# The opening of a two-part transformer: its first modulated features regrouped by fours, handed on one k-tile at a time

## The chip, the cores and the metric

The kernel runs on one core of a Trainium2 chip. The metric is device time in microseconds (us), from the first to the last instruction of the program plus what lies around them. Lower is better.

## The reference, cut to what matters

The program is a chain of two blocks on a sequence of 256 rows of 1024 features. The first block has two layers of adaptive modulation, a hybrid attention and a gated feed-forward part, the second two layers with attention and a squared-ReLU part. Only the very first steps are touched by the change:

```python
def rmsnorm(x, g):
    y = xf * lax.rsqrt(jnp.mean(xf * xf, axis=-1, keepdims=True) + RMS_EPS)
    return (y * g).astype(x.dtype)

cos, sin = rope_tables(positions)
cond = jax.nn.silu(c)
for l in range(DEPTH):
    mod = (cond @ ada_w[l] + ada_b[l])[:, None, :]
    sh1, sc1, g1, sh2, sc2, g2 = jnp.split(mod, 6, axis=-1)
    h = rmsnorm(x, norm1_g[l]) * (1 + sc1) + sh1
    x = x + g1 * hybrid_mixer(h, cos, sin, w_in[l], b_in[l], rel_bias[l], ...)   # starts with h @ w_in + b_in
    ...
```

Here `c` is one row of 1024, `ada_w[l]` is 1024 x 6144, `w_in[l]` is 1024 x 6733, and `h` is 256 x 1024. So the first product `h @ w_in` can't start before the row `cond @ ada_w` has given the shift (`sh1`) and the scale (`sc1`) of the features that it takes.

## The kernel before, in words

**Numbers and tiles.** A weight goes to TensorE as two rounded parts. ACT (ScalarE) copies a unit of the weight (two k-tiles of 128 rows, up to 512 columns) from `raw_units` to `hi_units` (line 1305), and POOL (GpSimd) writes the rest, raw minus hi, to `lo_units`, one k-tile at a time (line 730). The features are held turned (features on partitions) in `turned`, also as a hi and a lo part. Per k-tile and 128-row tile there are three matmuls (line 776): hi by hi, lo by hi, hi by lo. A unit is thus 12 matmuls, 8 on `hi_units` and 4 on `lo_units`. The eight input chunks of the first product are 458 columns wide; a chunk is 4 units. Chunks use two pairs of PSUM banks in turn, so the third chunk waits until DVE (VectorE) has drained the first (line 2025).

**Where the data comes from.** SP (SyncE) issues nearly all loads in one fixed order, the list `stream` of `plan()`: units of `ada_w` and of the weights, woven. Units of `w_in` go to 8 slots, and a slot is free when POOL has made its lo part.

**The opening.** The modulation of the first norm consists of four pieces of 512 features: scale0, shift0, scale1, shift1 (0 for features 0 to 511, 1 for the rest), each 4 units of 2 k-tiles of `ada_w`. DVE adds up the k-tiles of a piece over the partitions' own rows, one instruction of 128 x 512 each (lines 1714, 1717, 1720), the last one to `mod_rows`. The second unit of scale1 is left to TensorE (`PE_UNITS`, line 1113). Then TensorE adds over partitions and turns the sum to columns at once, with four matmuls of one column for a piece (`column_sums`, line 1123); an f32 matmul shows in the trace as two instructions. The bias row and the norm's gain are loaded as rows to one partition, and turned to columns with matmuls of one row (lines 1104 and 1097). The bias row of three pieces also enters DVE's first sum of a piece (line 1714), so it is loaded over memsets of POOL and DVE.

ACT meanwhile squares `x`, takes the root, and writes x over the root mean square to `o_rows` (`unit_rows`, line 1355), which TensorE transposes (line 909). `first_columns` (DVE, line 1794 on) and `first_hi` (ACT, line 1336 on) then scale and shift the turned features, two k-tiles at once: DVE scales the first pair, ACT the second, ACT makes the hi parts (line 1347), DVE the lo parts (line 1768), and TensorE starts on a pair when its lo part is there. Both run once for each half. Between the halves TensorE multiplies the first half's features with two units of chunk 0, and one or two units of chunk 1. The rotary angles and the table of the relative bias are made by DVE and ACT after the second half (`tables`, `angles`, lines 1945 to 1975; sine, line 1532).

`keep_running` (line 1131) issues full-width matmuls whose result nobody reads; it only gives TensorE something to do.

**Order.** Nothing is scheduled by a planner here: each engine's order is the order of its code, and engines wait on semaphores for named events. `sums_upto(n)` lets DVE go through the modulation units up to the nth.

## Time and profile before

| | us |
|---|---|
| median of 3 runs (1469.13 to 1471.74) | 1470.4 |
| the profiled execution | 1470.62 |
| its span, first to last instruction | 1468.8 |
| TensorE (PE) busy | 1443.4 (98%) |
| GpSimd (POOL) busy | 1198.3 (82%) |
| ScalarE (ACT) busy | 748.1 (51%) |
| VectorE (DVE) busy | 727.8 (50%) |

The profiled execution lasts 1.8 us longer than its span, and 0.2 us longer than the median of the runs. PE is busy for nearly the whole span, so idle time of another engine matters only where PE waits for it. The engines' shares are means over the whole program; the change concerns only its first 57 us.

### The profile page before, as it was taken

What the parts mean: (1) busy time and instruction counts of PE and PEld (TensorE: products, weight loads), DVE (VectorE), ACT (ScalarE), POOL (GpSimd) and SP (SyncE); (2) the same over time, 40 slices, a digit from 0 to 9 for tenths busy, and PEclk for the clock granted to TensorE, in tenths of its full rate; (3) what the DMA queues carried; (4) which work ended last, traced back from release to release, by engine and by line L of the source; (5) the groups of instructions that cost most, each with busy time, mean ns of one, the idle gap of its engine ahead of it and who ended that gap; (6) DMA issues with size and microseconds to landing.
All of it is one profiled execution on the core that took longest, in us unless ns stands there. A gap on an engine that the chain in (4) does not pass through costs nothing.

```text
span 1468.8 us, 21705 instructions
## 1 busy us (share of the span) xinstructions
PE 1443.4 (98%) x7684; PEld 1217.0 (83%) x7684; DVE 727.8 (50%) x1579; ACT 748.1 (51%) x1246; POOL 1198.3 (82%) x974
## 2 busy tenths in 40 slices
PE   7999999999999999999999999999999999999997
PEld 5898777899988988777888888888888888788886
DVE  7863654776634654745566214364650044655202
ACT  4435774644444445765544445465654345555441
POOL 2799989888878987558998989908999978489994
PEclk8999999999999999999999999999999999999999
DMA  9994557678885995337775665714566757256561
GB/s 362 387 357 158 188 177 225 230 299 309 306 276 184 398 313 182 116 102 235 235 247 183 192 204 169 230 43 157 190 199 199 217 157 223 65 171 201 190 201 55
DMA packets 149416, 313.37 MB, mean 213 GB/s; under 512 B 10918, under 2 KB 31802, under 8 KB 149307
## 3 DMA queue, kind: packets, MB, share of 16 engines
...
## 4 chain that ended last, share of the span: by engine, by line
PE 92%; DVE 4%; ACT 2%; POOL 1%; issue 1%; DMA 1%; SPq 0%; DVEq 0%; ACTq 0%
PE bank L776 57%; PE bank L821 12%; PE bank L822 8%; PE bank L819 5%; PE bank L1006 2%; PE bank L986 1%; PE bank L1022 1%; POOL lo_units L730 1%; PE bank L857 1%; PE bank L966 1%; DMA x_rows<-in_x 1%; PE bank L1009 1%; PE bank L953 1%; ACT hi_units L1305 0%; PE bank L955 0%
## 5 line engine op out<-in xcount | busy, mean ns | idle before, releaser
L730 POOL TENSOR_TENSOR lo_units<-raw_units,hi_units 128x512 fp32r<-128x512 f32 (+3 forms) x928 | 1151.2, 1279 | 243.9 <-ACT hi_units L1305 241.2
L1305 ACT ACTIVATE hi_units<-raw_units 128x1024 fp32r<-128x1024 f32 (+1 forms) x468 | 480.5, 1031 | 424.2 <-PE bank L776 262.8
L776 PE MATMUL bank<-hi_units,turned 128*128 128x512 f32 (+3 forms) x1600 | 439.1, 389 | 2.1 <-DVE turned L1768 1.3
L776 PEld LDWEIGHTS bank<-hi_units,turned 128*128 128x128 f32 x1600 | 293.0, 189 | 53.8 <-DVE turned L1768 2.9
L822 PE MATMUL bank<-turned,lo_units 128*128 128x256 f32 x1024 | 287.9, 281 | 0.0
L776 PE MATMUL bank<-hi_units,turned_wide 128*128 128x512 f32 x992 | 274.5, 391 | 0.0
L821 PE MATMUL bank<-turned,hi_units 128*128 128x512 f32 x736 | 258.7, 396 | 0.0
L776 PE MATMUL bank<-lo_units,turned 128*128 128x512 f32 (+3 forms) x800 | 253.3, 384 | 0.8 <-POOL lo_units L730 0.5
L776 PEld LDWEIGHTS bank<-hi_units,turned_wide 128*128 128x128 f32 x992 | 185.3, 188 | 38.5 <-issue 0.5
L822 PEld LDWEIGHTS bank<-turned,lo_units 128*128 128x128 f32 x1024 | 194.3, 190 | 0.2
L776 PEld LDWEIGHTS bank<-lo_units,turned 128*128 128x128 f32 x800 | 150.0, 188 | 30.4 <-POOL lo_units L730 3.6
L821 PEld LDWEIGHTS bank<-turned,hi_units 128*128 128x128 f32 x736 | 138.1, 188 | 32.7
L776 PE MATMUL bank<-lo_units,turned_wide 128*128 128x512 f32 x496 | 160.7, 389 | 0.0
L1720 DVE SCALAR_TENSOR_TENSOR bank<-ada_units,small,bank 128x512 f32<-128x512 f32 x148 | 111.8, 756 | 33.7 <-DMA ada_units<-in_ada_w 28.9
L776 PEld LDWEIGHTS bank<-lo_units,turned_wide 128*128 128x128 f32 x496 | 93.1, 188 | 19.6
L1786 DVE TENSOR_REDUCE bank<-bank 128x256 f32<-128x512 f32 x92 | 64.3, 699 | 84.3 <-PE bank L822 83.6
L819 PE MATMUL bank<-turned,hi_units 128*128 128x256 f32 x576 | 104.0, 283 | 0.0
L819 PEld LDWEIGHTS bank<-turned,hi_units 128*128 128x128 f32 x576 | 90.2, 192 | 0.6
L1652 ACT ACTIVATE mlp_relu<-bank 128x256 f32<-128x256 f32 x56 | 21.6, 386 | 59.4 <-DVE bank L1786 58.8
L2213 DVE SCALAR_TENSOR_TENSOR bank<-x_rows,bank 128x512 f32<-128x512 f32 x8 | 5.2, 693 | 88.8 <-PE bank L776 88.8
L1782 DVE TENSOR_TENSOR turned_wide<-bank,turned_wide 128x256 fp32r<-128x256 f32 x92 | 39.0, 424 | 14.6 <-ACT turned_wide L1367 11.8
L2226 DVE SCALAR_TENSOR_TENSOR bank<-x_rows,bank 128x512 f32<-128x512 f32 x8 | 5.6, 696 | 75.8 <-PE bank L776 75.6
...
## 6 DMA issues: line engine op xcount, KB each, us to landing
...
```

The costliest lines, as they stand in the source:

```text
L730: pool.tensor_tensor(LO[:, s, b, 0:w], RAW[:, u["slot"], b, 0:w], HI_[:, s, b, 0:w].bitcast(F32), ALU.subtract).then_inc(lo_ready.sem, lo_ ...
L776: ins = pe.matmul(BANK[2 * c["pair"] + t][:, 0:w], (A[a] if A is BT else A[:, a])[:, part, t * P:(t + 1) * P], W[:, s, b, 0:w], start=(i = ...
L819: pe.matmul(bank[:, 0:S], HI_[:, s, b, at:at + P], A[:, kt, part, :], start=kt == 0 and part == 0, stop=False)
L821: pe.matmul(bank[:, :], HI_[:, s, b, at:at + P], A[:, kt, :, :].rearrange("p two s -> p (two s)"), start=kt == 0, stop=False)
L822: ins = pe.matmul(bank[:, 0:S], LO[:, s, b, at:at + P], A[:, kt, 0, :], start=False, stop=kt == KT - 1)
L857: ins = pe.transpose(BANK[(TQ, TP)[n % 2]][:, j * P:(j + 1) * P], src[:, t, (4 * half + j) * P:(4 * half + j + 1) * P], con("ident"))
L1006: pe.matmul(score_bank(pipe, h + n)[:, 0:S], pipe["qk"][rows_, slot, P:S], kk[rows_, :], start=True, stop=True)
L1305: act.activation(HI_[:, s, 0:n, 0:w], RAW[:, u["slot"], 0:n, 0:w], ACT.Copy)\
L1652: act.activation(RTN[:, m % 4, :], BANK[(TQ, TP)[m % 2]][:, 0:S], ACT.Relu).then_inc(act_side.sem, act_side.mark(("relu tile", i, m)))
L1720: ins = v.scalar_tensor_tensor(total, raw[:, k, :], COND[:, kt:kt + 1], partial, ALU.mult, ALU.add)
L1782: tell(v.tensor_tensor(AT[:, n, 1, :], h, AT[:, n, 0, :].bitcast(F32), ALU.subtract), turned_lo, (tag, "tile", n))
L1786: return v.tensor_reduce(to, bank[:, :].rearrange("p (two s) -> p s two", two=2), AX_X, ALU.add)
```

## The change

- **Fours.** Within a half, k-tile number j (0 to 3) now holds the features 4q + j, q being the partition, instead of 128j + q. The rows of `w_in` of layer 0 are loaded in the same order, `unit_rows` reads x with a step of four elements, and the last sum of each modulation piece is written to `mod_rows` in this order.
- **Columns.** With that, a partition's four biases (and gains) are four neighbours in memory, and two small loads put them into place as columns (`BIAS`, `GAIN`). The bias and gain matmuls, the row tile with its memsets, and the bias in DVE's first sum are gone. `scale_columns` makes the gain column from the sums of a scale piece before the shift piece is there, and `column_sums` of the shift follows it.
- **Scale1's unit on TensorE** is now two matmuls of 512 columns into one row (`sum_row`), which ACT writes to SBUF, regrouped, and four matmuls of one row turn it to columns.
- **Single k-tiles.** `first_hi`, `first_columns` and the new `first_unit` hand over one k-tile at a time; two k-tiles of a half share each of the two banks. All eight transposes of a half are issued together (`first_turn`).
- **Order.** `tables`, `angles`, the sines and the store of the bias table come first on DVE and ACT. On PE, chunk 1's second unit moves ahead of the column sums of shift1. There are 15 `keep_running` matmuls in place of 6.

The diff, cut to its core:

```diff
-                    a = tile_rows(src)[row0:row0 + ((n - 1) * step + 1) * P, col0:col0 + ncols].rearrange("(k p) n -> p k n", p=P)[:, ::step, :]
+                    if src == ("w_in", 0):
+
+                        half, j = divmod(row0 // P, 4)
+                        a = tile_rows(src)[half * CW:(half + 1) * CW, col0:col0 + ncols].rearrange("(q j) n -> q j n", j=4)[:, j:j + n, :]
+                    else:
+                        a = tile_rows(src)[row0:row0 + ((n - 1) * step + 1) * P, col0:col0 + ncols].rearrange("(k p) n -> p k n", p=P)[:, ::step, :]
...
-        def column_products(c, i):
+        def sum_row(c, i):
 
             u = c["units"][i]
             pe.wait_ge(ada_in[u["home"]][u["slot"]], 16 * (u["turn"] + 1))
             for k in range(UNIT_K):
+                kt = i * UNIT_K + k
+                ins = pe.matmul(BANK[3][0:1, :], COND[:, kt:kt + 1], ada_raw(u)[:, k, :], start=k == 0, stop=k == UNIT_K - 1)
             ins.then_inc(ada_multiplied.sem, ada_multiplied.mark(u["index"]))
...
             pe.wait_ge(ada_used.sem, ada_used.at(c["units"][-1]["index"]))
+            if n == 3:
+                for j in range(4):
+                    pe.matmul(columns[:, at + j:at + j + 1], SUM_ROW[0:1, j * P:(j + 1) * P], ONES[0:1, 0:1], start=j == 0, stop=False)
+            if n < 2:
+                pe.wait_ge(rows.sem, rows.at(("scales", half)))
             for j in range(4):
                 ins = pe.matmul(columns[:, at + j:at + j + 1], MOD[:, n * CW + j * P:n * CW + (j + 1) * P], ONES[:, 0:1],
-                                start=False, stop=n < 2 and j == 3)
-            if n < 2:
-                ins.then_inc(product.sem, product.mark(("columns", half)))
-
-        def keep_running(n):
+                                start=n != 3 and j == 0, stop=j == 3)
+            ins.then_inc(product.sem, product.mark(("columns", n)))
...
+        def first_turn(half):
+
+            pe.wait_ge(act_side.sem, act_side.at(("unit rows", half)))
+            if half:
+                for k in (2, 3):
+                    pe.wait_ge(turned_lo.sem, turned_lo.at((("n1", 0), k)))
+            for k in range(4 * half, 4 * half + 4):
+                for t in range(NT):
+                    at = k % 4 // 2 * S + t * P
+                    ins = pe.transpose(BANK[(TQ, TP)[k % 2]][:, at:at + P], O[:, t, k * P:(k + 1) * P], con("ident"))
...
+        def first_unit(c, i):
+
+            for m in range(UNIT_K):
+                pe.wait_ge(turned_lo.sem, turned_lo.at((("n1", 0), i * UNIT_K + m)))
+                unit(c, i, HT, only=m)
...
-        keep_running(1)
-        pe.wait_ge(first_gain_in, 16)
-        gain_columns(0)
-        pe.wait_ge(first_bias_in, 16)
-        bias_columns(scale0)
-        keep_running(2)
+        keep_running(6)
         column_sums(scale0)
+        keep_running(4)
...
-                ready = lambda g: (act_side, ("unit rows", g // 2))
-                turn(tag, O, range(4), 0, ready)
-                turn(tag, O, range(4), 1, ready)
+                first_turn(0)
                 keep_running(1)
                 column_sums(shift0)
                 keep_running(2)
-                for i in (0, 1):
-                    pe.wait_ge(turned_lo.sem, turned_lo.at((tag, i)))
-                    unit(c0, i, HT)
-                turn(tag, O, range(4), 2, ready)
-                turn(tag, O, range(4), 3, ready)
-                pe.wait_ge(rows.sem, rows.at(("columns", 0)))
-                gain_columns(1)
-                column_products(scale1, 1)
+                first_unit(c0, 0)
+                first_unit(c0, 1)
+                sum_row(scale1, 1)
+                first_turn(1)
+                pe.wait_ge(act_side.sem, act_side.at("sum row"))
                 unit(c1, 0, HT)
                 column_sums(scale1)
+                unit(c1, 1, HT)
                 column_sums(shift1)
-                unit(c1, 1, HT)
-                for c in (c0, c1):
-                    for i in (2, 3):
-                        pe.wait_ge(turned_lo.sem, turned_lo.at((tag, i)))
-                        unit(c, i, HT)
+                keep_running(2, BANK[SB_[0]])
+                first_unit(c0, 2)
+                first_unit(c0, 3)
+                unit(c1, 2, HT)
+                unit(c1, 3, HT)
...
+            a, b, c, d = range(4 * half, 4 * half + 4)
+            raw = lambda k: BANK[(TQ, TP)[k % 2]][:, k % 4 // 2 * S:(k % 4 // 2 + 1) * S]
+
+            def whole(k):
+                act.activation(raw(k), raw(k), ACT.Identity, scale=GAINED[:, k:k + 1], bias=SHIFT[:, k:k + 1])\
+                    .then_inc(act_side.sem, act_side.mark(("whole", k)))
+
+            def hi(k, signal_):
+                act.wait_ge(signal_.sem, signal_.at(("whole", k)))
+                act.activation(HT[:, k, 0, :], raw(k), ACT.Copy).then_inc(turned_hi.sem, turned_hi.mark((("n1", 0), k)))
+
+            act.wait_ge(turned.sem, turned.at((("n1", 0), half)))
             act.wait_ge(rows.sem, rows.at(("columns", half)))
+            whole(b)
+            hi(a, rows)
+            hi(b, act_side)
+            hi(c, rows)
+            act.wait_ge(turned_lo.sem, turned_lo.at((("n1", 0), b)))
+            whole(d)
+            hi(d, act_side)
...
-                ins = act.activation(O[:, t, cols], X[:, t, cols], ACT.Copy, scale=RR[:, t:t + 1])
+                ins = act.activation(O[:, t, cols].rearrange("p (j q) -> p j q", j=4), X[:, t, cols].rearrange("p (q j) -> p j q", j=4),
...
+        act.dma_start(GAIN.rearrange("p (h j) -> p h j", h=2), dram["norm1_g"][0:1, :].rearrange("a (h q j) -> (a q) h j", h=2, j=4),
+                      allow_slow_non_contiguous=True).then_inc(first_gain_in, 16)
+        act.dma_start(BIAS.rearrange("p (c j) -> p c j", c=4), dram["ada_b"][0:1, 0:4 * CW].rearrange("a (c q j) -> (a q) c j", c=4, j=4),
+                      allow_slow_non_contiguous=True).then_inc(first_bias_in, 16)
-        act.dma_start(GAIN_ROW, dram["norm1_g"][0:1, :]).then_inc(first_gain_in, 16)
-        act.wait_ge(cleared.sem, cleared.at("second shift"))
-        act.wait_ge(rows.sem, rows.at("cleared"))
-        act.dma_start(FIRST[0:1, :], dram["ada_b"][0:1, 0:4 * CW]).then_inc(first_bias_in, 16)
+        for what, dst in (("sin", SIN), ("cos", COS)):
+            act.wait_ge(rows.sem, rows.at(what))
+            act.activation(dst, dst, ACT.Sin).then_inc(act_side.sem, act_side.mark(what))
+        act.wait_ge(rows.sem, rows.at("rel"))
+        act.dma_start(scratch[:, :], RE[:, :]).then_inc(scratch_in, 16)
...
+                prep(3)
+                act.wait_ge(ada_multiplied.sem, ada_multiplied.at(by_key["ada", 0, 3]["units"][1]["index"]))
+                act.activation(SUM_ROW[0:1, :].rearrange("p (j q) -> p q j", j=4), BANK[3][0:1, :].rearrange("p (q j) -> p q j", j=4), ACT.Copy)\
+                    .then_inc(act_side.sem, act_side.mark("sum row"))
                 prep(NH)
                 first_hi(1)
                 prep(NH + 3)
...
-                    if kt == 0 and (u["l"], u["c"]) in FIRST_BANK and (u["l"], u["c"]) != (0, 2):
-                        dve.wait_ge(cleared.sem, cleared.at("second shift"))
-                        dve.wait_ge(first_bias_in, 16)
-                        link(v.scalar_tensor_tensor(partial, raw[:, k, :], COND[:, kt:kt + 1], FIRST[:, cols], ALU.mult, ALU.add))
-                        continue
                     if kt == 0:
                         link(v.tensor_scalar(partial, raw[:, k, :], COND[:, kt:kt + 1], None, ALU.mult))
                         continue
                     total = MOD[:, cols] if (u["i"], k) == (mine[-1], UNIT_K - 1) and not in_two(u["l"], u["c"]) else partial
+                    if (u["l"], u["c"]) in FIRST_BANK and total is not partial:
+                        by_four = lambda a: a.rearrange("p (q j) -> p q j", j=4)
+                        ins = v.scalar_tensor_tensor(total.rearrange("p (j q) -> p q j", j=4), by_four(raw[:, k, :]), COND[:, kt:kt + 1], by_four(partial),
+                                                     ALU.mult, ALU.add)
...
+            dve.wait_ge(product.sem, product.at(("columns", 2 + half)))
+            dve.wait_ge(first_bias_in, 16)
+            dve.wait_ge(first_gain_in, 16)
+            link(v.scalar_tensor_tensor(GAINED[:, cols], columns[:, at], 1.0, BIAS[:, at], ALU.add, ALU.add))
+            say(v.tensor_tensor(GAINED[:, cols], GAINED[:, cols], GAIN[:, cols], ALU.mult), ("scales", half))
...
         def first_columns(half):
+            a, b, c, d = range(4 * half, 4 * half + 4)
+            raw = lambda k: BANK[(TQ, TP)[k % 2]][:, k % 4 // 2 * S:(k % 4 // 2 + 1) * S]
+
+            def whole(k):
+                say(v.tensor_scalar(raw(k), raw(k), GAINED[:, k:k + 1], SHIFT[:, k:k + 1], ALU.mult, ALU.add), ("whole", k))
+            def lo(k):
+                dve.wait_ge(turned_hi.sem, turned_hi.at((("n1", 0), k)))
+                tell(v.tensor_tensor(HT[:, k, 1, :], raw(k), HT[:, k, 0, :].bitcast(F32), ALU.subtract), turned_lo, (("n1", 0), k))
-            link(v.tensor_copy(GAIN[:, cols], columns[:, 2 * KT + 4 * half:2 * KT + 4 * half + 4]))
-            v.tensor_copy(SHIFT[:, cols], columns[:, cols])
-            say(v.scalar_tensor_tensor(GAINED[:, cols], columns[:, KT + 4 * half:KT + 4 * half + 4], 1.0, GAIN[:, cols], ALU.add, ALU.mult),
-                ("columns", half))
-            g = 2 * half
-            dve.wait_ge(turned.sem, turned.at((("n1", 0), g)))
-            for k in (2 * g, 2 * g + 1):
-                part = BANK[TQ][:, k % 2 * S:(k % 2 + 1) * S]
-                ins = v.tensor_scalar(part, part, GAINED[:, k:k + 1], SHIFT[:, k:k + 1], ALU.mult, ALU.add)
-            say(ins, ("whole", half))
-            turn_lo(("n1", 0), HT, part=slice(2 * half, 2 * half + 2))
+            say(v.tensor_tensor(SHIFT[:, cols], columns[:, cols], BIAS[:, cols], ALU.add), ("columns", half))
+            dve.wait_ge(turned.sem, turned.at((("n1", 0), half)))
+            whole(a)
+            lo(a)
+            lo(b)
+            whole(c)
+            lo(c)
+            lo(d)
...
-        say(v.memset(FIRST[:, 2 * CW:4 * CW], 0.0), "cleared")
...
+        tables()
+        angles()
         sums_upto(5)
+        scale_columns(0)
+        sums_upto(6)
         dve.wait_ge(act_side.sem, act_side.at(("root", ("n1", 0))))
         say(v.reciprocal(RR[:, 0:NT], RSTD), "inverse root")
         sums_upto(8)
         for l in range(DEPTH):
             if l == 0:
                 first_columns(0)
+                sums_upto(13)
+                scale_columns(1)
                 sums_upto(15)
                 first_columns(1)
-                tables()
-                angles()
```

TensorE (PE) from the start of the program to the first products; L1131 and L1139 are `keep_running`, L1123 and L1114 the column sums, L909 and L1127 the transposes. Before:

```order
L1131 MATMUL bank<-ada_units_61,constants 128x512
L1097 MATMUL bank<-ones_rounded,bias_masks 128x1 x4
L1104 MATMUL bank<-ones_rounded,first_biases 128x1 x4
L1131 MATMUL bank<-ada_units_61,constants 128x512 x2
L1123 MATMUL bank<-ones_rounded,mod_rows 128x1 x4
L909 MATMUL bank<-constants,o_rows 128x128 x8
L1131 MATMUL bank<-ada_units_61,constants 128x512
L1123 MATMUL bank<-ones_rounded,mod_rows 128x1 x4
L1131 MATMUL bank<-ada_units_61,constants 128x512 x2
L776 MATMUL bank<-hi_units,turned 128x458 x4
```

The same place on PE, now:

```order
L1139 MATMUL bank<-ada_units_61,constants 128x512 x6
L1114 MATMUL bank<-ones_rounded,mod_rows 128x1 x4
L1139 MATMUL bank<-ada_units_61,constants 128x512 x4
L1127 MATMUL bank<-constants,o_rows 128x128 x8
L1139 MATMUL bank<-ada_units_61,constants 128x512
L1114 MATMUL bank<-ones_rounded,mod_rows 128x1 x4
L1139 MATMUL bank<-ada_units_61,constants 128x512 x2
L776 MATMUL bank<-hi_units,turned 128x458 x4
```

The one-row matmuls for gain and bias are gone, and full-width matmuls without use stand in their place.

DVE at the start; `small` holds all small columns, `rel_extended` is the table of the relative bias. Before:

```order
L1938 MEMSET first_biases 128x1024
L1941 SCALAR_TENSOR_TENSOR small<-small 128x8
L1942 TENSOR_SCALAR small<-small 128x8
L1944 TENSOR_SCALAR ones_rounded<-constants 128x128
L1717 TENSOR_SCALAR bank<-ada_units_61,small 128x512
```

The same place on DVE, now (eight more small rows like the last but one stand before the last):

```order
L1974 TENSOR_SCALAR ones_rounded<-constants 128x128
L1979 TENSOR_SCALAR rel_extended<-rel_rows 10x256
L1980 TENSOR_SCALAR rel_extended<-rel_rows 10x128
L1986 CAST small<-positions_int 128x2
L1988 TENSOR_SCALAR small<-constants,small 128x8 x2
L1995 TENSOR_SCALAR small<-small 128x16
```

The fourteen instructions of the tables and angles stand ahead of the first sum of a modulation piece.

DVE in the second half; the first rows are sums of shift1 and the last of them writes `mod_rows`. Before:

```order
L1720 SCALAR_TENSOR_TENSOR bank<-ada_units_67,small,bank 128x512 x5
L1720 SCALAR_TENSOR_TENSOR mod_rows<-ada_units_67,small,bank 128x512
L1799 COPY small<-bank 128x4
L1800 COPY small<-bank 128x4
L1801 SCALAR_TENSOR_TENSOR small<-bank,small 128x4
```

The same place on DVE, now:

```order
L1734 SCALAR_TENSOR_TENSOR bank<-ada_units_67,small,bank 128x512 x2
L1816 SCALAR_TENSOR_TENSOR small<-bank,small 128x4
L1817 TENSOR_TENSOR small<-small 128x4
L1734 SCALAR_TENSOR_TENSOR bank<-ada_units_67,small,bank 128x512 x3
L1731 SCALAR_TENSOR_TENSOR mod_rows<-ada_units_67,small,bank 128x128x4
L1833 TENSOR_TENSOR small<-bank,small 128x4
L1826 TENSOR_SCALAR bank<-bank,small 128x256
```

`scale_columns` (L1816, L1817) now stands between sums of shift1, and waits there for PE's column sums of scale1.

## Rows read from the trace of the kernel before

**Rows 1.** The page: busy us, share, instructions; granted PE clock by fortieths.

```profile
PE 1443.4 (98%) x7684; PEld 1217.0 (83%) x7684; DVE 727.8 (50%) x1579; ACT 748.1 (51%) x1246; POOL 1198.3 (82%) x974
```

**Rows 2.** Timeline, first 7 us: start, us, engine, line, operation [idle before <-releaser].

```profile
1.36 0.42 ACTq L1504 DMA_DIRECT2D positions_int<-in_positions  x1
1.81 1.28 ACT L1507 ACT_TABLE_LOAD   x1 [1.81 <-issue]
...
3.87 0.23 DVE L1944 TENSOR_SCALAR ones_rounded<-constants 128x128 fp32r<-128x128 f32 x1
...
6.13 0.75 DVE L1717 TENSOR_SCALAR bank<-ada_units,small 128x512 f32<-128x512 f32 x1 [2.04 <-DMA ada_units<-in_ada_w]
```

**Rows 3.** Timeline of the first half, 15 to 25 us.

```profile
15.09 0.95 PE L1123 MATMUL bank<-ones_rounded,mod_rows 128*128 128x1 f32 x8
15.80 2.56 ACT L1355 ACTIVATE o_rows<-x_rows,small 128x512 f32<-128x512 f32 x4 [0.30 <-DVE small L1981]
15.80 3.92 DVE L1720 SCALAR_TENSOR_TENSOR bank<-ada_units,small,bank 128x512 f32<-128x512 f32 x5
17.19 1.09 PE L909 MATMUL bank<-constants,o_rows 128*128 128x128 f32 x8 [1.14 <-ACT o_rows L1355]
19.16 0.97 ACT L1305 ACTIVATE hi_units<-raw_units 128x916 fp32r<-128x916 f32 x1 [0.79 <-DMA raw_units<-in_w_in]
23.00 1.00 DVE L1807 TENSOR_SCALAR bank<-bank,small 128x256 f32<-128x256 f32 x2
```

**Rows 4.** Chain of waits, 20 to 41 us: start, us, what.

```profile
20.56 1.87 PE bank L1123 x8
22.43 3.26 PE bank L1131 x4
25.69 5.07 PE bank L776 x24
30.75 0.88 PE bank L909 x8
...
32.61 1.88 PE bank L1113 x16
34.48 3.89 PE bank L776 x12
38.38 1.98 PE bank L1123 x16
```

**Rows 5.** Timeline, 43 to 57 us.

```profile
43.40 0.72 PEld L776 LDWEIGHTS bank<-hi_units,turned 128*128 128x128 f32 x4 [0.83 <-DVE turned L1768]
47.54 2.23 DVE L1958 TENSOR_SCALAR small<-constants,small 128x8 f32<-128x8 f32 x2
52.20 0.17 DVE L1974 SCALAR_TENSOR_TENSOR small<-small 128x16 f32<-128x16 f32 x1
54.06 6.88 POOL L730 TENSOR_TENSOR lo_units<-raw_units,hi_units 128x458 fp32r<-128x458 f32 x6 [3.19 <-ACT hi_units L1305]
54.10 0.71 PEld L776 LDWEIGHTS bank<-hi_units,turned 128*128 128x128 f32 x4 [0.82 <-DVE proj_rows L2025]
55.30 0.30 PEld L776 LDWEIGHTS bank<-lo_units,turned 128*128 128x128 f32 x2 [0.49 <-POOL lo_units L730]
56.87 0.81 PEld L776 LDWEIGHTS bank<-hi_units,turned 128*128 128x128 f32 x4
```

**Rows 6.** Windows: stretch, length, busy by engine, granted PE clock, DMA share, GB/s.

```profile
18.70:25.00 6.30, 5.51 (x14) 2.88 (x12) 3.40 (x9) 3.90 (x6) 4.50 (x4) 0.50 1.05 405
```

**Rows 7.** DMA, first 6 us: packets, MB, share of 16 engines.

```profile
q10 hardware_dynamic: 294, 0.02, 3.7%
```

**Rows 8.** The page's costliest groups: xcount | busy, mean ns | idle before.

```profile
L1786 DVE TENSOR_REDUCE bank<-bank 128x256 f32<-128x512 f32 x92 | 64.3, 699 | 84.3 <-PE bank L822 83.6
L1652 ACT ACTIVATE mlp_relu<-bank 128x256 f32<-128x256 f32 x56 | 21.6, 386 | 59.4 <-DVE bank L1786 58.8
L1782 DVE TENSOR_TENSOR turned_wide<-bank,turned_wide 128x256 fp32r<-128x256 f32 x92 | 39.0, 424 | 14.6 <-ACT turned_wide L1367 11.8
```

45 lines of the change are left out of this document (10 added, 35 removed).

## The prediction

> **What bounds the kernel now.** I read the page first. PE is busy for 98% of the span, POOL, the next, for 82% [rows 1]. So the place to look is the opening, where PE has little to multiply; what is won there passes on to the end only if it brings PE's unbroken stretch forward. The timeline shows where that stretch begins: PE waits last for the drain of chunk 0 and for a lo part, and from 56.87 us (the second unit of chunk 2) it goes on without a hole [rows 5]. Hence the measure for every step below: when does this same unit begin?
>
> Before it, the chain of waits shows what PE is held by [rows 4]. It waits for the modulation of each half, and fills the time with useless matmuls: the first product starts at 25.69. In the second half the column sums end at 40.36 (38.38 + 1.98), and the next product starts at 43.40 [rows 5]. DVE sums the whole time, 0.785 us an instruction (3.92 for five) [rows 3]. The third view is the granted clock: 0.50 from 18.7 to 25.0 [rows 6], the lower of its two levels (1.2 of 2.4 GHz); PE had been through one-column matmuls and a wait of 1.14 us just before [rows 3].
>
> **The start.** Two loads more are issued on ACT ahead of its first table. One like them takes 0.42, 0.47 with the gap, so the table, at 1.81 before, comes at 2.75, and DVE's last preparing instruction, which ended at 4.10, ends at 5.05 [rows 2]. Then DVE has 14 small instructions. Beside POOL they took 1.11 each (2.23 for two), the later ones 0.17 [rows 5]; POOL is idle this early, so I count 0.21 each with the gap, 2.95. Bounds: 2.4 to 15.6 (14 x 0.17, 14 x 1.11); I take the low side because POOL has no unit yet. DVE's first sum is at 8.0, against 6.13 [rows 2].
>
> The two loads consist of 768 runs of 16 bytes. In the first 6 us 294 packets of ACT's queue took 3.7% of 16 engines, 3.55 us in all, 12 ns each [rows 7]; 768 make 9.2, or 0.6 us for each of the 16. So the data may come 0 to 0.6 later. DVE, itself 1.9 late, is what the first half then waits for, so I take nothing. The memsets and the bias and gain matmuls of the first half that go are worth nothing either: they lay under waits for the modulation.
>
> **First half.** From 8.0: ten sums to 15.85, two small instructions of `scale_columns` (0.4), two sums, the reciprocal (0.2) at 18.0, four sums to 21.15. Before, the last sum ended at 20.5 (five from 15.80 in 3.92, and one more) [rows 3]; the idle 2.04 and the wait for the root that DVE had are what pays for the tables. `unit_rows` starts at 18.05 instead of 15.80 and takes 2.56 [rows 3]; the first half of it is there at 19.35, the transposes (1.09) end at 20.4, one `keep_running` at 21.3, and the column sums at 22.25. Before that was 22.43 [rows 4], no gain. That sum takes the faster clock: column sums cost 0.95 at it and 1.87 at the slower [rows 3, 4]; a `keep_running` is two instructions, 1.63 to 1.7 in the slow stretch (3.26 for four) [rows 4] and half of it in the fast one.
>
> Here the single k-tiles pay. Before, DVE's small ones, two scalings (1.00), two ACT copies of 512 and a lo part lay between the sums and the first product. Now ACT has the two first units to copy (0.97 each [rows 3]) until 22.6, one scaling 0.5, one copy of 256 columns at 0.39 and one lo part of 256 at 0.42 [rows 3, 8]: 24.0, just when two fast `keep_running` end. First product at 24.0 instead of 25.69: 1.7 won. POOL's lo parts (1.15 each: 6.88 for six) [rows 5] are ready from 22.85 on.
>
> **Second half.** PE, one after the other: four k-tiles 5.07 [rows 4], to 29.1; `sum_row`, two f32 matmuls of 512 columns, priced as `keep_running` at the fast clock, 1.7, to 30.8 (bounds 0.8 and 3.4, half and twice); eight transposes, 1.0 (0.88 to 1.09) [rows 3, 4], to 31.8; a unit, 2.5 (half of 5.07), to 34.3; column sums of scale1, now eight matmuls or 16 instructions, 1.98 as for the 16 before [rows 4], to 36.3. DVE meanwhile: its last lo part at 26.7 (the other three k-tiles take 2.7 more), and ten sums, to 34.55. Then it must wait for those columns until 36.3, for 1.8 us, with the last four sums of shift1 queued behind it: this is the new wait. 0.4 for the scale and four sums, 3.14, bring it to 39.9, and PE, which waits for them, has the column sums at 40.85. Before: 40.36. So half a microsecond is lost here, and of the 1.7 nothing is left.
>
> From there: two `keep_running` (1.7), the product at 42.6, against 43.40: 0.8 won by the single k-tiles again. But ACT is held longer: 0.2, two scalings, four copies of 0.39 and its waits for DVE's end 3.9 after the columns; then it copies the unit for k-tiles 6 and 7 until 45.8, where PE wants it at 45.1. Its lo part takes 1.15 more and is wanted after two thirds of a k-tile, 0.83: that is 0.7 and 0.35, 1.05 lost.
>
> **The tables' old place.** They no longer stand between the second half and the drain of chunk 0, nor the sine before ACT's copies. Both waits of PE there go: four units from 43.40 on and one more, at 2.5, would have brought it to 55.9, and it was 56.87, so they cost 0.97 [rows 5]. What is late next is POOL's lo part of chunk 2's first unit, at 53.9 with 54.5 wanted: hidden.
>
> **Sum.** Product at 42.6, 10.0 for four units, 1.05 of stalls, 2.5 for the first unit of chunk 2: 56.15, against 56.87. 0.7 us won. The profiled execution lasts 1470.62, so 1469.9; the median of the runs is 0.2 lower, so 1469.7. A change of 0.2% is 2.9 us, about what a measurement of this kernel can tell from none: the forecast is no change.
>
> **A rule that speaks against it.** `unit_rows` now reads x in steps of 16 bytes, and four last sums write in steps of 512. No SBUF access of this kind is in the trace. The nearest row is L1786, which reads PSUM in steps of 1 KB: 699 ns for 512 elements, as fast as neighbours would be [rows 8]. So I take no cost. Bounds: nothing to twice the duration, 2.56 and 4 x 0.75 more.
>
> The Trainium skill, page "SBUF — State Buffer", section "Door 1: The DMA port swizzle", says that SBUF has lines of 16 bytes, and that an access that crosses to a new line pays. By it each element of `unit_rows` would pay; by the row none does. No run here shows it yet.
>
> **Rivals.**
> - *No new wait (18%).* DVE isn't held for scale1's columns, because PE gets there 1.8 earlier: `sum_row` at its low bound, or the units at less than I count. For it: the sum on PE is long, and each term can be short. Against: these terms are measured rows but for one. It gives 1.8 more: 1467.9.
> - *The clock falls again (20%).* It fell to 1.2 GHz after one-column matmuls and a wait, and from 18.7 on cost 6.3 us at half speed [rows 6]. Such stretches are still there: transposes and column sums from 19.3 to 22.3, and 38.8 to 40.9, where PE waits for DVE. Against: `keep_running` lies between. Price: column sums 0.9 and two `keep_running` 1.7 longer in the first half, 2.6, or about 1.7 in the second. I take 2.1: 1471.8. That the clock would stay low from the start is unlikely: column sums at 15.09 were fast [rows 3], after 3.5 us of full-width work, and now 5 to 10 us of it come first.
> - *Stepped access is slow (12%).* Where: ACT's four `unit_rows` and DVE's last sum of each piece. At twice the duration, two writes put the reciprocal and shift0 0.75 and 1.5 back, `unit_rows` adds 2.56: first product 3.3 later; shift1's last sum adds 0.75. 4.05 on 1469.7 is 1473.75, slower than before by 3.3. It decides from a factor of 1.2 on (all 0.7 gone), and passes 0.2% at 1.9. For it: the rule; against it: L1786.
> - That the change doesn't do what it says I rule out: the order of instructions shows each move.
>
> **How the numbers follow.** Forecast 50%, own range 1468.5 to 1471.0 (the stalls of 1.05 in or out, as much again for the small terms). No new wait 18%, clock 20%, steps 12%. Faster by over 0.2% (under 1467.5): half of the first rival, and the forecast's lower tail, 17%. Slower (over 1473.3): 8% from the steps and 3% from a clock that falls twice, 11%. The rest, 72%, within 0.2%. The range that leaves out two in ten is 1467.2 to 1472.3.
>
> **What would show it.** DVE's fourteen small instructions at 0.2 and a first sum near 8.0; `unit_rows` at 2.56 in all, and the last sums at 0.75; first products near 24.0; an idle time of DVE near 1.8 before `scale_columns(1)`, released by PE; ACT late with one unit at 45; no wait of PE at the start of chunk 2; and that chunk's second unit near 56.15. Wrong it would be if POOL or the loads, which run at 405 GB/s here [rows 6], can't follow a PE that is 0.8 ahead: then a hole opens after 57 us that wasn't there. It would also be wrong if the clock is at 0.5 from 22 to 25 or at 41.

## The result, and the profile after

The changed kernel takes 1475.9 us (median of 20 runs, 1474.5 to 1477.5); the kernel before, beside it, 1471.45 (most runs 1470 to 1473). Ratio 1.0027, 95% interval 1.0019 to 1.0035: about 4 us slower, where 0.7 us faster was forecast and the range ended at 1472.3. The profiled execution has a span of 1473.6 us against 1468.8.

PE's share is what it was, 98% [rows 1], so I look at the opening first:

```profile
PE 1446.2 (98%) x7674; PEld 1214.0 (82%) x7674; DVE 722.8 (49%) x1582; ACT 751.2 (51%) x1251; POOL 1196.2 (81%) x972
```

The timeline of PE after (start, us, engine, line, operation, idle before), the rows that answer to [rows 3 to 5]:

```profile
15.04 1.05 PE L1114 MATMUL bank<-ones_rounded,mod_rows 128*128 128x1 f32 x8 [1.00 <-DVE mod_rows L1731]
...
21.14 1.09 PE L1127 MATMUL bank<-constants,o_rows 128*128 128x128 f32 x8 [1.51 <-ACT o_rows L1364]
...
26.34 1.09 PE L776 MATMUL bank<-hi_units,turned 128*128 128x458 f32 x4 [0.65 <-DVE turned L1830]
...
43.49 1.05 PE L1114 MATMUL bank<-ones_rounded,mod_rows 128*128 128x1 f32 x8 [1.56 <-DVE mod_rows L1731]
44.41 2.76 PE L1139 MATMUL bank<-ada_units,constants 128*128 128x512 f32 x4
46.40 2.30 PE L776 MATMUL bank<-hi_units,turned 128*128 128x458 f32 x4
...
49.08 1.00 PE L776 MATMUL bank<-hi_units,turned 128*128 128x458 f32 x4
...
60.33 1.00 PE L776 MATMUL bank<-hi_units,turned 128*128 128x458 f32 x4
```

The last row is chunk 2's second unit, from which PE goes on without a hole. Its first matmul was at 57.07 before (its weight loads at 56.87 [rows 5]), so the opening is 3.26 us longer. Three marks are used from here on: the **first product** (26.34; before 25.69 by the chain [rows 4], 25.48 by the timeline; forecast 24.0), the **product of k-tile 4** (46.40; 43.40; 42.6), and this **last mark** (60.33; 57.07; forecast 56.35, which is 56.15 for its loads).

DVE and ACT, same columns:

```profile
8.34 0.75 DVE L1726 TENSOR_SCALAR bank<-ada_units,small 128x512 f32<-128x512 f32 x1
...
13.88 1.10 DVE L1731 SCALAR_TENSOR_TENSOR mod_rows<-ada_units,small,bank 128x512 f32<-128x512 f32 x1
...
21.14 1.16 DVE L1731 SCALAR_TENSOR_TENSOR mod_rows<-ada_units,small,bank 128x512 f32<-128x512 f32 x1
...
39.43 0.16 DVE L1816 SCALAR_TENSOR_TENSOR small<-bank,small 128x4 f32<-128x4 f32 x1 [1.99 <-PE bank L1114]
```

```profile
18.77 4.56 ACT L1364 ACTIVATE o_rows<-x_rows,small 128x512 f32<-128x512 f32 x4 [2.92 <-DVE small L2015]
```

`unit_rows` takes 4.56 instead of 2.56 [rows 3] and a last sum 1.10 to 1.16 instead of 0.75. The wait of 1.99 is the new wait that was forecast as 1.8. The stretches show the clock (length, busy by engine, granted clock, DMA):

```profile
44.00:46.00 2.00, 2.00 (x8) 1.12 (x9) 0.79 (x3) 1.09 (x3) 0.00 (x0) 0.86 1.05 403
46.00:48.00 2.00, 2.00 (x5) 1.22 (x4) 1.41 (x4) 0.67 (x3) 0.00 (x0) 0.50 1.04 400
48.00:50.00 2.00, 2.00 (x9) 1.75 (x9) 0.76 (x2) 1.97 (x4) 0.42 (x1) 0.79 1.05 405
```

So three suspects stand in one trace: the steps (stepped accesses), the wait (DVE for scale1's columns) and the clock. The chain of waits (start, us, what) runs through all three:

```profile
19.99 3.34 ACT o_rows L1364 x3
...
33.45 1.10 ACT first_sum_row L1544
...
38.35 1.00 PE bank L1114 x8
...
42.35 1.10 DVE mod_rows L1731
...
43.49 1.05 PE bank L1114 x8
44.55 2.62 PE bank L1139 x4
```

### The profile page after: what moved, and what is told of

Same layout as the page of the kernel before. It is cut to its first block, busy times and chain, and to the rows that moved or that the text cites. A ratio compares the mean times of both kernels' runs of the same rounds, so it can differ in the third digit from the quotient of the medians.

```text
span 1473.6 us, 21699 instructions
## 1 busy us (share of the span) xinstructions
PE 1446.2 (98%) x7674; PEld 1214.0 (82%) x7674; DVE 722.8 (49%) x1582; ACT 751.2 (51%) x1251; POOL 1196.2 (81%) x972
## 4 chain that ended last, share of the span: by engine, by line
PE 92%; DVE 4%; ACT 2%; issue 1%; POOL 1%; ACTq 0%; DVEq 0%
PE bank L776 58%; PE bank L821 12%; PE bank L822 8%; PE bank L819 5%; PE bank L1006 2%; PE bank L986 1%; POOL lo_units L730 1%; PE bank L1022 1%; PE bank L966 1%; DVE bank L1734 1%; PE bank L857 1%; PE bank L1009 1%; ACT hi_units L1305 1%; PE bank L953 0%; PE bank L909 0%
## 5 line engine op out<-in xcount | busy, mean ns | idle before, releaser
L821 PE MATMUL bank<-turned,hi_units 128*128 128x512 f32 x736 | 260.1, 398 | 0.0
L821 PEld LDWEIGHTS bank<-turned,hi_units 128*128 128x128 f32 x736 | 138.3, 188 | 33.8
```

The source lines that it names most:

```text
L821: pe.matmul(bank[:, :], HI_[:, s, b, at:at + P], A[:, kt, :, :].rearrange("p two s -> p (two s)"), start=kt == 0, stop=False)
```

## Experiments

The marks come from each kernel's one profiled execution, the medians from 5 to 12 runs (probe: one), the ratio is against the kernel before with its 95% interval. "Clock low" is where it was at 0.50 after 12 us. All values are in us. unit_flat, sums_flat, both_flat, flat_kept and probe leave regrouping out, so they compute something else and serve for times only.

| kernel | first product | k-tile 4 | last mark | clock low | median | ratio |
|---|---|---|---|---|---|---|
| before | 25.48 | 43.40 | 57.07 | 18.4-25.2, 35.4-38.8 | 1471.45 | 1 |
| changed | 26.34 | 46.40 | 60.33 | 45.4-48.8 | 1475.9 | 1.0027 |
| unit_flat | 25.71 | 46.55 | 59.73 | 16.4-19.8, 43.7-47.1 | 1475.8 | 1.0023 (1.0010-1.0036) |
| sums_flat | 25.99 | 45.68 | 59.60 | 44.9-48.3 | 1475.0 | 1.0021 (1.0008-1.0034) |
| both_flat | 25.34 | 46.62 | 60.93 | 15.5-18.9, 39.4-49.6 | 1474.8 | 1.0016 (1.0002-1.0029) |
| scale_late | 26.34 | 44.65 | 58.34 | none | 1473.8 | 1.0013 (1.0001-1.0025) |
| warm | 26.34 | 46.42 | 60.10 | none | 1475.9 | 1.0023 (1.0011-1.0034) |
| tables_late | 26.00 | 47.62 | 62.71 | 19.8-23.2, 40.3-50.5 | 1477.9 | 1.0036 (1.0023-1.0049) |
| tables_kept | 25.45 | 46.71 | 62.58 | 39.2-42.6 | 1478.3 | 1.0039 (1.0027-1.0052) |
| before_tables | 25.41 | 48.90 | 61.40 | 18.2-28.4, 35.2-48.9 | 1470.3 | 0.9999 (0.9986-1.0012) |
| probe | 24.93 | 45.10 | 59.00 | 44.4-47.8 | 1473.4 | one run |
| pe_late | 26.05 | 48.98 | 62.67 | 39.3-46.1 | 1479.3 | 1.0040 (1.0023-1.0057) |
| flat_kept | 24.77 | 46.03 | 59.72 | 38.5-42.0 | 1475.0 | 1.0019 (1.0010-1.0028) |
| twos | 24.55 | 44.98 | 58.24 | 42.3-45.7 | 1473.7 | 1.0018 (1.0010-1.0027) |
| twos_warm | 24.63 | 44.37 | 58.06 | none | 1473.9 | 1.0016 (1.0007-1.0024) |
| twos_no_prep | 24.54 | 42.35 | 56.04 | none | 1472.5 | 1.0011 (1.0002-1.0020) |
| twos_all | 25.27 | 43.30 | 55.90 | none | 1471.6 | 0.9991 (0.9980-1.0002) |
| twos_seven | 24.54 | 43.90 | 56.50 | 37.1-40.6 | 1471.3 | 0.9997 (0.9986-1.0007) |
| fours_all | 26.36 | 46.16 | 58.77 | 39.5-42.9 | 1473.2 | 1.0012 (1.0003-1.0022) |

**The steps, taken away.** unit_flat, sums_flat, and both_flat with the two edits:

```diff
-                ins = act.activation(O[:, t, cols].rearrange("p (j q) -> p j q", j=4), X[:, t, cols].rearrange("p (q j) -> p j q", j=4),
-                                     ACT.Copy, scale=RR[:, t:t + 1])
+                ins = act.activation(O[:, t, cols], X[:, t, cols], ACT.Copy, scale=RR[:, t:t + 1])
...
-                        ins = v.scalar_tensor_tensor(total.rearrange("p (j q) -> p q j", j=4), by_four(raw[:, k, :]), COND[:, kt:kt + 1], by_four(partial),
-                                                     ALU.mult, ALU.add)
```

> ACT's four unit_rows read x as it lies instead of in steps of 16 bytes (the output is then not the reference's: x isn't regrouped). Theory S (stepped access is what put the first half back): the four take 2.56 as in the kernel before instead of 4.56, the transposes begin about 1.0 earlier (20.1 instead of 21.14), the first product about 0.7 earlier (25.6; the column sums of shift0, held by DVE's sums that end at 22.30, bound it), and so does everything behind: 1475.9 - 0.7 = 1475.2. Rival W (only the new wait of DVE and the clock behind it cost): the four are faster, but the second half, where DVE's sums bound, begins as before: no change, 1475.9. Both expect DVE's wait of about 2 and the clock at 0.5 near 45 to stay.

> DVE's four last sums write MOD as it lies instead of in steps of 512 bytes (the modulation is then not regrouped, the output not the reference's). Theory S: each takes 0.75 instead of 1.10 to 1.16, the reciprocal comes 0.35 earlier (18.2), shift0's sum 0.75 earlier (21.55); the first product about 0.4 earlier (ACT's unit_rows of 4.56 then bounds it), the end of shift1's sums 1.4 earlier only if DVE's wait for scale1's columns doesn't take it up; forecast 1475.9 - 0.7 = 1475.2. Rival W: these sums are hidden by the wait of 2.0 behind them, no change: 1475.9.

> Both at once: no stepped access on ACT or DVE but for the one row of sums (the output is not the reference's). Theory S: first product at about 24.0 to 24.5 as forecast (26.34 now), scale1's columns 1.9 earlier, DVE's wait for them stays near 1.8, PE's clock falls behind it as now: 1475.9 - 2.1 = 1473.8. If the clock does not fall, 1472.3. Rival W: the steps cost under 0.5: 1475.4 or more.

The first product came 0.63, 0.35 and 1.0 earlier, the last mark 0.60 and 0.73 earlier and, with both, 0.60 later. By the marks the single edits side with theory S, that the steps cost time; by the medians they decide little, and unit_flat's 1475.8 is even its rival's number. The pair doesn't agree with S: its clock fell at 15.5, and again at 39.4, about 1 us behind the sixteen one-column matmul instructions for scale1's columns, where PE had no idle time at all, and there it stayed low for 10.2 us instead of 3.4.

**What a step costs.** In probe the four `unit_rows` have four forms, and so have the four last sums.

> What an access of each form costs, in the changed kernel's own instructions (the output is not the reference's). ACT, 512 f32 an instruction: as it lies; read in steps of 8 bytes; read in steps of 16; written in steps of 16. DVE, last sums of 512: as it lies; both reads in steps of 16; written in steps of 16; written in steps of 8 (the changed kernel's are written in steps of 512 bytes: 1.10 to 1.16). If what counts is the line of 16 bytes that each element must open: 16 bytes slow (1.14 on ACT, 1.1 to 1.2 on DVE), 8 bytes half as much more (0.9 on ACT, 0.93 on DVE), writes on ACT as slow as reads. Rival (any access that isn't contiguous pays the same): 8 bytes as slow as 16. Rival (reads pay on ACT, writes on DVE only): ACT's write 0.64, DVE's reads 0.75.

ACT, two instructions a row: the first row holds the contiguous form and a read in steps of 8 bytes, the second a read in steps of 16 and a write in steps of 16.

```profile
18.40 1.36 ACT L1374 ACTIVATE o_rows<-x_rows,small 128x512 f32<-128x512 f32 x2 [2.88 <-DVE small L2026]
```

```profile
19.67 2.34 ACT L1374 ACTIVATE o_rows<-x_rows,small 128x512 f32<-128x512 f32 x2
```

One by one they take 0.72, 0.73, 1.23 and 1.20. DVE, in this order: contiguous, both reads in steps of 16, write in steps of 16, write in steps of 8:

```profile
13.87 0.75 DVE L1743 SCALAR_TENSOR_TENSOR mod_rows<-ada_units,small,bank 128x512 f32<-128x512 f32 x1
...
20.78 1.14 DVE L1743 SCALAR_TENSOR_TENSOR mod_rows<-ada_units,small,bank 128x512 f32<-128x512 f32 x1
...
31.73 1.20 DVE L1743 SCALAR_TENSOR_TENSOR mod_rows<-ada_units,small,bank 128x512 f32<-128x512 f32 x1
...
41.39 0.75 DVE L1743 SCALAR_TENSOR_TENSOR mod_rows<-ada_units,small,bank 128x512 f32<-128x512 f32 x1
```

Here steps of 8 bytes are free to within 0.01 (in twos, whose `unit_rows` take 0.76 each where the kernel before has 0.71, to within 0.05), and steps of 16 make an instruction 1.5 to 1.7 times as long, read or written, on both engines; the changed kernel's writes in steps of 512 (1.10 to 1.16) cost about the same. DVE's two reads, one from SBUF and one from a bank, were stepped together, so which of them pays isn't shown. The first theory expected half the price for 8 bytes; at the two widths measured it is none or all. The Trainium skill, page "SBUF — State Buffer", section "Door 1: The DMA port swizzle", says that two accesses to a line of 16 bytes are enough for the full rate and that each crossing to a new line pays. By that rule 8-byte steps are free; the probe agrees.

**The wait.** scale_late:

```diff
-                sums_upto(13)
-                scale_columns(1)
                 sums_upto(15)
+                scale_columns(1)
```

> The two instructions that take scale1's columns stand behind all of shift1's sums on DVE, instead of ahead of its last four; nothing else changes, the result is the same. Theory W (the new wait of DVE of 2.0 opens PE's idle time of 1.56, and the clock falls to 0.5 behind it): shift1's sums end at 41.1 instead of 43.4, PE goes on without idle time from c1's second unit (41.9), and the product of k-tile 4 is there at 44.9 instead of 46.4, with the clock at 1.0, which keeps 1.5 more: 1475.9 - 3.0 = 1472.9. Rival C (the clock falls through the one-column matmuls themselves, wait or not): only the 1.5 are won, the clock stays at 0.5 for some 3 us: 1474.4. Theory S alone expects 1475.9 (nothing).

k-tile 4 came at 44.65 (1.75 earlier), the last mark 1.99 earlier, and no low clock was left. Theory W, that the new wait costs time, held for the wait; of its further 1.5 for the clock only 0.24 appeared by the last mark (1.99 less 1.75). Behind k-tile 5 PE now waited for ACT's copy.

**The clock.** warm fills PE's idle time:

```diff
                 unit(c1, 1, HT)
+                pe.wait_ge(rows.sem, rows.at(("scales", 1)))
+                for _ in range(2):
+                    pe.matmul(columns[:, 64:CW], con("ident"), ada_raw(scale0["units"][0])[:, 0, 64:CW], start=True, stop=True)
                 column_sums(shift1)
```

> The changed kernel with two useless matmuls more (448 columns each, f32, into the bank of the columns) where PE waits for shift1's last sum (1.56 idle, 41.9 to 43.5); they wait first for DVE to have read scale1's columns (40.0), which costs nothing. Theory C2 (the clock falls at 45.7 because PE did little from 36 to 43.5: one-column matmuls and idle time): filled, the clock stays at 1.0, the two keep_running behind take 1.96 instead of 2.76 and the first k-tile 1.25 instead of 2.5; product of k-tile 4 at 45.6, chunk 2 2.0 earlier (58.1 instead of 60.1): 1475.9 - 2.0 = 1473.9. Rival (the clock falls at a moment that PE's idle time has no part in, as it did in the kernel with both steps gone, at 39 right behind sixteen one-column matmuls): it falls all the same, no change or up to 0.5 worse: 1475.9 to 1476.4.

PE's timeline in warm:

```profile
46.42 1.10 PE L776 MATMUL bank<-hi_units,turned 128*128 128x458 f32 x4
...
47.77 1.00 PE L776 MATMUL bank<-hi_units,turned 128*128 128x458 f32 x4
...
49.67 1.07 PE L776 MATMUL bank<-hi_units,turned 128*128 128x458 f32 x4 [0.48 <-ACT hi_units L1308]
...
51.36 1.00 PE L776 MATMUL bank<-hi_units,turned 128*128 128x458 f32 x4
```

The clock was kept, and only 0.23 of the expected 2.0 came. The two fast k-tiles (4 and 5) run into ACT's copy of the next unit: 47.77 to 51.36 is 3.59 for two k-tiles of 1.25, so 1.09 of stall. In the changed kernel that stall lay hidden under the slow k-tile. The faster `keep_running` won nothing either, since k-tile 4 started at 46.4 in both: DVE's lo part, which it needs, ended just ahead of that in both.

**Tables first.** tables_late puts `tables()`, `angles()`, sines and store back behind the second half; tables_kept adds three `keep_running` ahead of the first transposes and the filler of warm. before_tables does this one part of the change in the kernel before:

```diff
+        tables()
+        angles()
         sums_upto(5)
...
                 first_columns(1)
-                tables()
-                angles()
```

> The changed kernel with the fourteen small instructions of tables and angles, the two sines and the scratch store back in their old place behind the second half. DVE's first sum then waits for its load (6.2 instead of 8.34), so shift0's last sum ends at 20.2 instead of 22.3 and the first product comes at 24.2 instead of 26.34; shift1's sums come 2.1 earlier too if the clock behaves; the old place costs what it cost before, about 1.0 (PE waits again for the drain of chunk 0). Theory: 1475.9 - 2.1 + 1.0 = 1474.8, so tables first was a loss of about 1, not a gain. Rival (my forecast's step: DVE had the time to spare in the first half, tables first wins 1.0): first product no earlier than 25.8, total 1476.4. Whether the clock falls in it is open and worth 1.7 either way.

> The changed kernel with tables, angles and sines in their old place, as before, but with 7 keep_running instead of 4 ahead of the first transposes and two of 448 columns ahead of shift1's column sums, where the clock fell. Theory (tables first costs the first half what DVE doesn't have: its load is there at 5.9 and it starts at 8.34): with the clock kept the first product comes at 24.8 instead of 26.34, product of k-tile 4 at 45.0, ACT's stall 1.1 stays, and PE waits 1.2 for chunk 0's drain as the late tables made it before: chunk 2's second unit at 60.0 against 60.10 with tables first and the clock kept: tables first is worth nothing. Rival (my forecast's step: it is worth 1.0): 61 or later.

> The kernel before with one part of the change alone: tables, angles, the two sines and the scratch store stand first instead of behind the second half. The result is the same. Theory (the forecast's step): DVE's first sum moves from 6.13 to 7.2 and its idle time of 1.59 ahead of the reciprocal takes that up, so the first half ends as before (column sums of shift0 at 22.4), the first product stays at 25.7, and PE no longer waits for chunk 0's drain: chunk 2's second unit at 56.1 instead of 57.07, 1 us faster. Rival (DVE's loads came as it needed them, and it is now 1.1 late for all of it): first product 0.5 to 1.1 later, nothing won.

I was wrong on the first two. In tables_late DVE did start at 5.87 and finished shift0 1.4 earlier, but the first product came only 0.34 earlier (0.89 in tables_kept), and PE then waited where chunk 2 begins, for 0.8 in tables_late and 2.2 in tables_kept, where the changed kernel and warm have no wait. So the rival (the forecast's step) was right. Both also had the clock low behind scale1's columns, which is part of why their k-tile 4 is later. In before_tables the first half is not later (25.41), and k-tile 4 to the last mark takes 12.50, against 13.67 in the kernel before: that is ten k-tiles of 1.25 without a stall, so all of the 1.17 of waits is gone (0.97 in the forecast, which counted to the weight loads). The slow clock gave DVE and ACT about 1.5 more time ahead of k-tile 4 there, but the drain of chunk 0 ended at 55.38, 3.5 ahead of chunk 2's start at 58.90. Its profiled execution, 1476.9 us, had the clock low for 23.9 us where the kernel before had 10.2:

```profile
38.00:40.00 2.00, 2.00 (x7) 1.75 (x6) 0.35 (x1) 0.00 (x0) 0.00 (x0) 0.50 1.06 418
40.00:42.00 2.00, 2.00 (x9) 1.85 (x9) 0.00 (x0) 0.00 (x0) 0.00 (x0) 0.50 1.02 399
42.00:44.00 2.00, 2.00 (x11) 2.00 (x11) 0.00 (x0) 0.00 (x0) 0.00 (x0) 0.50 1.05 405
```

The median of its runs is 1470.3 and the interval holds 1, so a gain of 1 us is neither shown nor excluded in the total.

Why the old place costs is in the kernel before, DVE's timeline (start, us) beside POOL's:

```profile
49.80 1.10 DVE L1965 TENSOR_SCALAR small<-small 128x16 f32<-128x16 f32 x1
50.94 0.17 DVE L1966 TENSOR_SCALAR small<-small 128x16 f32<-128x16 f32 x1
```

```profile
43.97 6.90 POOL L730 TENSOR_TENSOR lo_units<-raw_units,hi_units 128x458 fp32r<-128x458 f32 x6 [5.22 <-ACT hi_units L1305]
```

While POOL makes lo parts, the first small instructions take 1.05 to 1.20 each; from POOL's end at 50.87 on they take 0.17. ACT's sines wait for them, 5.08 before the first, and ACT's copies of the weights stand behind the sines. In the first place the same instructions take 0.17 to 0.28, with POOL idle.

**PE takes the steps.** pe_late leaves ACT and DVE contiguous, lets PE read in steps of 16 bytes, and takes scale1's columns late as scale_late does:

```diff
-                    ins = pe.transpose(BANK[(TQ, TP)[k % 2]][:, at:at + P], O[:, t, k * P:(k + 1) * P], con("ident"))
+                    ins = pe.transpose(BANK[(TQ, TP)[k % 2]][:, at:at + P], O[:, t, half * CW + k % 4:(half + 1) * CW:4], con("ident"))
...
-                ins = pe.matmul(columns[:, at + j:at + j + 1], MOD[:, n * CW + j * P:n * CW + (j + 1) * P], ONES[:, 0:1],
+                ins = pe.matmul(columns[:, at + j:at + j + 1], MOD[:, n * CW + j:(n + 1) * CW:4], ONES[:, 0:1],
```

> All regrouping is moved to PE's reads: unit_rows, the last sums and the copy of the row of sums are contiguous; the transposes, the column sums and the sum row's columns read every fourth column (steps of 16 bytes); and scale1's columns are taken behind shift1's sums. The result is the same. Theory: PE reads such steps at no cost (transposes 1.09 for eight, column sums 0.95 to 1.05), so all that the steps cost on ACT and DVE is won, 2.0 + 4 x 0.35, and DVE's wait too: shift1's sums end near 40, product of k-tile 4 near 43 if the clock stays, ACT's copies then hold PE for about 1: chunk 2's second unit at 56.5 to 57, total 1472. Rival P (PE pays for the steps as ACT does, a factor of 1.7): transposes 1.9 and column sums 1.7, most of them on the path, 3 x 0.8 + 2 x 0.8: 4 lost against that: 1475 or more. The clock can fall in either, for 1.7.

```profile
14.69 2.03 PE L1114 MATMUL bank<-ones_rounded,mod_rows 128*128 128x1 f32 x8 [0.38 <-DVE mod_rows L1728]
...
20.38 1.24 PE L1127 MATMUL bank<-constants,o_rows 128*128 128x128 f32 x8
```

Rival P was right for the column sums: weights loaded in steps of 16 bytes make them 2.03 instead of 1.05 (1.89 instead of 0.95), while the transposes take 1.24 instead of 1.09. It was the slowest kernel; a clock that was low from 39.3 to 46.1 is part of that.

**Without the steps, in the change's own order.** flat_kept is both_flat with 8 `keep_running` instead of 6 at the start and warm's filler. twos deals features in twos (2q and 2q+1 of each 256), so every step is 8 bytes:

```diff
-                ins = act.activation(O[:, t, cols].rearrange("p (j q) -> p j q", j=4), X[:, t, cols].rearrange("p (q j) -> p j q", j=4),
+                ins = act.activation(O[:, t, cols].rearrange("p (j r) -> p j r", j=2), X[:, t, cols].rearrange("p (r j) -> p j r", j=2),
...
-  a = tile_rows(src)[half * CW:(half + 1) * CW, col0:col0 + ncols].rearrange("(q j) n -> q j n", j=4)[:, j:j + n, :]
+  a = tile_rows(src)[half * CW:(half + 1) * CW, col0:col0 + ncols].rearrange("(g q j) n -> q g j n", g=2, j=2)[:, g:g + n, j, :]
```

> The changed kernel in its own order with neither stepped access on ACT's unit_rows nor on DVE's last sums (the output is not the reference's), and with useless matmuls where the clock was seen to fall: 8 keep_running instead of 6 ahead of the first column sums, and two of 448 columns ahead of shift1's. Theory (the forecast's sum holds once steps and clock are taken out): first product at 24.2 (forecast 24.0), DVE's wait for scale1's columns 1.8, product of k-tile 4 at 43.2, ACT holds PE for 1.1 behind it (forecast 1.05), chunk 2's second unit at 56.8 against 57.07 before and 60.33 in the changed kernel; total 1471.4, as before. Rival (something else in the change costs as well, the loads or a longer chain on PE): the product of k-tile 4 at 44.5 or later with the clock at 1.0 throughout.

> Features are dealt in twos instead of fours: a partition gets features 2q and 2q+1 of each 256, so every stepped access (unit_rows, last sums, the row of sums) reads in steps of 8 bytes; loads of w_in and of biases and weights follow. The result is the same, the order of work that of the changed kernel. Theory (each access pays for a new line of 16 bytes, 8 bytes are free as in the probe: 0.73 on ACT, 0.75 on DVE): unit_rows 2.6 to 2.9, last sums 0.75 to 0.8, so all falls out as with both steps gone: first product 25.3 with the clock lost in the first half, 24.3 with it kept. Total 1473 to 1475.5 by the clock. Rival (a read in steps of 8 bytes through three dimensions costs as the 16 did): 1475.9 and unit_rows above 4.

> Twos, in the changed kernel's own order, with the two useless matmuls of 448 columns ahead of shift1's column sums that kept the clock before; the result is the same. Theory (the forecast's sum, once the steps are free and the clock kept): first product 24.6, DVE's wait for scale1's columns 2.0, product of k-tile 4 at 43.3 (44.98 in twos, where the clock fell at 42.3), ACT's stall of 1.1 comes to light behind it, chunk 2's second unit at 57.0 (58.24 in twos, 57.07 before): 1471.5, as before. Rival (the clock falls earlier instead, as with both steps gone): 58 to 59.7.

flat_kept missed: the clock fell at 38.5 all the same, and the filler then cost time (shift1's last sum ended at 41.58, and PE came to its columns at 43.23). In twos `unit_rows` takes 2.74 and the last sums 0.75; the last mark comes 2.09 earlier than in the changed kernel. twos_warm, with the clock kept, has the terms of the forecast's own sum:

```profile
24.63 1.09 PE L776 MATMUL bank<-hi_units,turned 128*128 128x458 f32 x4
...
37.06 1.07 PE L776 MATMUL bank<-hi_units,turned 128*128 128x458 f32 x4
...
41.46 1.05 PE L1114 MATMUL bank<-ones_rounded,mod_rows 128*128 128x1 f32 x8
...
44.37 1.09 PE L776 MATMUL bank<-hi_units,turned 128*128 128x458 f32 x4
```

My 43.3 for it was 1.1 too early, since I took the low clock in twos to cost more than it did.

**The repairs.** twos_all is twos with scale1 late, 8 `keep_running` first, and `prep(NH + 1)` instead of `prep(NH)` ahead of `first_hi(1)`; twos_seven has 7, twos_no_prep leaves the last edit out, fours_all has the three repairs with features in fours.

> Twos, and the three repairs together: scale1's columns behind shift1's sums, 8 keep_running ahead of the first column sums, and ACT copies chunk 0's last unit ahead of the second half's columns, not behind them. The result is the same. Theory: first product 24.3, shift1's sums end at 39, PE goes on without idle time, product of k-tile 4 at 42.6, no stall for ACT's copies behind it, chunk 2's second unit at 55.3 against 57.07 before: 1471.5 - 1.8 = 1469.7. Rival (ACT's copy waits for its load, since 404 GB/s is all that comes in): the stall of 1.1 stays in another place, 1470.8. Rival (the clock falls all the same): 1471 to 1473.

> The kernel of twos with three repairs, but ACT copies chunk 0's last unit where the changed kernel does, behind the second half's features. Theory (forecast: ACT late for k-tiles 6 and 7, 0.7 and 0.35): PE waits 1.1 there with the clock kept: chunk 2's second unit at 57.0 instead of 55.90. Rival (POOL or the loads hold PE at 55.9 anyway): 56.2 or less.

> The kernel of twos with three repairs, but 7 keep_running instead of 8 ahead of the first column sums: with 8, DVE waited 0.77 for PE there. Theory: that wait goes, all behind it comes 0.6 earlier: product of k-tile 4 at 42.7, chunk 2's second unit at 55.3 (55.90 with 8, 57.07 before), 1471.0 or less. Rival (a short idle time of PE at 14.2 is enough for the clock to fall): 56.5 or later.

> The three repairs (scale1's columns behind shift1's sums, 8 keep_running first, the last unit copied earlier) on the changed kernel with its features in fours and so its steps of 16 bytes. The result is the same. Theory (steps cost unit_rows 1.8 and the last sums 0.35 each, on the path as long as DVE and ACT are what PE waits for): first product 26.4, product of k-tile 4 at 44.7 to 45.2, chunk 2's second unit at 57.3 to 57.8 against 55.90 in twos: 1.4 to 1.9 for the steps alone, 1472.5 to 1473. Rival (with the repairs the steps are hidden behind PE's work): 56.4 or less.

Stall: k-tile 4 to the last mark takes 13.69 without the early copy (twos_no_prep) and 12.60 with it (twos_all), 1.09. The last marks differ by 0.14 only, for a reason that has no part in the copy: twos_all's first `keep_running` went at the slow pace (0.85 an instruction instead of 0.43) until some 11, in twos_no_prep until some 9, so the eight together took 10.16 instead of 8.72, ended behind DVE's first sums, and its first product came 0.73 later. Wait: twos_no_prep against twos_warm, k-tile 4 at 42.35 and 44.37, 2.02. (twos_no_prep has no filler, and eight `keep_running` where twos_warm has six; they end ahead of the first sums.) Steps: fours_all against twos_no_prep has the first product 1.82 later; its last mark, about 1 us later than forecast, also holds a low clock, so it says less. twos_seven had its first product 0.73 ahead of twos_all and lost that to a low clock at 37.1. twos_all stands at 0.9991 of the kernel before, the changed kernel at 1.0027, and the intervals are apart; against the kernel before its own, 0.9980 to 1.0002, just holds 1.

## Why the prediction was wrong

What failed is the step "So I take no cost" for the stepped accesses: they cost 2.0 us. Beside it the sum for the rest was 1.7 us too short in many small terms. By the last mark, in single traces:

- *Steps.* warm 60.10, twos_warm 58.06: **2.04** (medians 1475.9 and 1473.9). The bound of 2.56 for `unit_rows` and 0.75 for a sum was double the duration; measured are 2.00 and 0.35 to 0.41. The rival "stepped access is slow" had 12% and the right place. L1786, on which I relied, reads PSUM, and says nothing of SBUF. That twos also loads `w_in` in another order is not what won the time: flat_kept loads it as the changed kernel does, and has its first product at 24.77.
- *The own sum.* twos_warm 58.06 against a forecast of 56.35: **1.71**. The first product is 0.63 late (first sum at 8.37, not 8.0; the rest adds 0.26). PE's chain to scale1's columns takes 12.6, not 12.3. From there to shift1's last sum 4.2, not 3.6: a small instruction of DVE takes 0.75 while POOL is at work, and I counted 0.2. From there to k-tile 4 2.95, not 2.7; I had PE's `keep_running` as what it waits for, and DVE's lo part is there no earlier.
- *The clock.* changed 60.33, warm 60.10: **0.23**. The rival had 20% and a price of 1.7 for this half. The fall came, at 45.4, behind the place where PE waits for DVE, but the price didn't, since ACT's stall takes its place.
- Together 3.98: from 56.35 to 60.33.

Right were: the new wait (1.8 forecast, 1.99 measured), and that it eats what the single k-tiles win; taking it away won 2.0 (twos_warm against twos_no_prep). ACT's stall: 1.05 forecast, 1.09 measured, though in the changed kernel it is not to be seen. The tables' old place: the waits there are gone, 0.97 counted to the weight loads, 1.17 to the matmuls. The hole that was named as a sign of being wrong is one wait of 0.3 for POOL between 150 and 300 us, which the kernel before doesn't have.

Of the 4.4 us between the medians, 3.3 are in the opening. Of the rest, some 1.3 arises in the changed kernel's profiled execution between about 1040 and 1100 us, where PE waits for nothing and its L821 matmuls take 399 ns instead of 391 (171 of them). In warm and twos_all it is 399 too, in scale_late 394; the change doesn't touch that place, and the cause is open.
